# A ninth 2 MB buffer for expert weights in a two-layer hybrid decoder step

## What is computed

```python
def moe(h, router_w, router_bias, w_gate, w_up, w_down):
    score = jax.nn.sigmoid((h @ router_w).astype(jnp.float32))
    ...
    gate = (jax.nn.one_hot(idx, N_EXPERTS, dtype=jnp.float32) * w[..., None]).sum(-2).astype(h.dtype)
    out = jnp.zeros_like(h)
    for e in range(N_EXPERTS):
        hid = jax.nn.silu(h @ w_gate[e]) * (h @ w_up[e])
        out = out + gate[..., e:e + 1] * (hid @ w_down[e])
    return out

def layer_tail(x, mix, p_i, ln1_g, ln1_b, ln2_g, ln2_b, router_w, router_bias, w_gate, w_up, w_down, ple_proj, ple_gate):
    h = layer_norm(DEEPNORM_ALPHA * x + mix, ln1_g, ln1_b)
    h = layer_norm(DEEPNORM_ALPHA * h + moe(h, router_w, router_bias, w_gate, w_up, w_down), ln2_g, ln2_b)
    return h + jax.nn.sigmoid(h @ ple_gate) * (p_i @ ple_proj)
```

## Time and profile before

| | us |
|---|---|
| median of three runs | 1065.74 |
| lowest and highest run | 1064.29, 1072.47 |
| span of the profiled execution | 1061.0 |
| PE busy | 1002.3 (94%) |
| PEld busy | 626.2 (59%) |
| DVE busy | 489.0 (46%) |
| ACT busy | 334.2 (32%) |
| POOL busy | 186.5 (18%) |
| moved by DMA | 343.32 MB, mean 324 GB/s |

### The profile page before, as it was taken

How to read it: one execution, slowest core, us unless ns; L and a number is a source line. 1 busy time by engine, 2 the same in 40 slices (tenths; PEclk the granted TensorE clock), 3 DMA queues, 4 the chain that set the end, 5 groups by cost and what they waited for, 6 DMA issues and landing times. The chain is left out here.

```text
span 1061.0 us, 15018 instructions
## 1 busy us (share of the span) xinstructions
PE 1002.3 (94%) x5207; PEld 626.2 (59%) x5207; DVE 489.0 (46%) x1423; ACT 334.2 (32%) x874; POOL 186.5 (18%) x201
## 2 busy tenths in 40 slices
PE   8999999899999999989999987979999999998997
PEld 6888776688744444433678865445874444443366
DVE  1869898782531111101479896671152111110146
ACT  3211688920351111101241013662045111110134
POOL 0000005330130000000245542441112000000033
PEclk9999999999999999999999996999989999999999
DMA  9844688769669999999837995949966999999975
GB/s 328 289 148 167 175 270 276 244 228 401 255 266 428 425 429 425 427 426 426 342 134 261 385 342 178 333 143 361 424 257 248 424 427 426 427 425 426 429 305 212
DMA packets 89985, 343.32 MB, mean 324 GB/s; under 512 B 15826, under 2 KB 53714, under 8 KB 72978
## 3 DMA queue, kind: packets, MB, share of 16 engines
q1 hardware_dynamic: 79914, 319.58, 77.5%
q10 hardware_dynamic: 7688, 18.39, 4.7%
q0 software_dynamic: 2304, 4.33, 1.2%
HBM read 331.66 MB, written 23.04 MB: 334 GB/s over the span
## 5 line engine op out<-in xcount | busy, mean ns | idle before, releaser
L1517 DVE TENSOR_TENSOR gates_and_hidden<-bank,silu_gate 128x512 f32<-128x512 f32 x16 | 11.1, 691 | 318.0 <-PE bank L1166 318.0
L547 PE MATMUL ss<-xT,expert_ring 128*128 128x264 f32 x384 | 92.4, 402 | 4.3 <-DMA expert_ring<-in_ssd_w_in 4.2
L1166 PE MATMUL bank<-expert_ring,x_packed 128*64 128x512 f32 x384 | 86.8, 596 | 7.4 <-DMA expert_ring<-in_moe_w_up 7.4
L1188 PE MATMUL bank<-expert_ring,gates_and_hidden 128*64 128x512 f32 x384 | 85.0, 595 | 1.4 <-ACT gates_and_hidden L1337 1.4
L547 PEld LDWEIGHTS ss<-xT,expert_ring 128*128 128x128 f32 x384 | 75.0, 198 | 18.7 <-DMA xT<-in_xT 4.2
L1147 PE MATMUL bank<-expert_ring,x_packed 128*64 128x512 f32 x384 | 84.5, 593 | 0.0
L1376 POOL DMA_INDIRECT x_rows_packed<-x_rows,slot_token_int x16 | 16.4, 1023 | 338.3 <-DVE gates_and_hidden L1480 294.7
L1510 DVE TENSOR_TENSOR acc<-acc,bank 128x264 f32<-128x264 f32 x128 | 55.0, 429 | 38.9 <-PE bank L1203 37.3
L1759 PE MATMUL bank<-xT,expert_ring 128*128 128x264 f32 (+1 forms) x324 | 72.5, 386 | 0.3 <-PEq L1000 0.3
L1759 PEld LDWEIGHTS bank<-xT,expert_ring 128*128 128x128 f32 (+1 forms) x324 | 60.3, 187 | 12.4 <-issue 1.0
L1203 PE MATMUL bank<-gates_and_hidden,y_slots 128*128 128x264 f32 x256 | 60.6, 388 | 3.8 <-issue 2.4
(11 more groups left out here) (417 smaller groups left out, 1760.4 us busy)
## 6 DMA issues: line engine op xcount, KB each, us to landing
expert_ring<-in_moe_w_down SPq DMA_DIRECT2D x24, 2048.0 KB, 21.9
expert_ring<-in_moe_w_gate SPq DMA_DIRECT2D x24, 2048.0 KB, 18.2
expert_ring<-in_moe_w_up SPq DMA_DIRECT2D x20, 2048.0 KB, 22.6
expert_ring<-in_ssd_w_in SPq DMA_DIRECT2D x9, 2048.0 KB, 8.0
expert_ring<-in_cmp_pages SPq DMA_DIRECT2D x40, 256.0 KB, 4.5
expert_ring_b<-in_moe_w_gate SPq DMA_DIRECT2D x4, 2048.0 KB, 20.2
expert_ring_c<-in_moe_w_gate SPq DMA_DIRECT2D x4, 2048.0 KB, 24.7
expert_ring<-in_moe_w_up SPq DMA_DIRECT2D x8, 1024.0 KB, 6.7
```

The lines of the kernel that those rows point to most:

```text
L547: last = mm(pt[m % 4][:, 0:T], wc[:, k, ((m - 1) % 4) * P:((m - 1) % 4 + 1) * P], xT[:, k, :], start=k == 0, stop=k == KD - 1)
L1166: last = mm(hb[1][s * CAP:(s + 1) * CAP, :], xg[:, k, s * CAP:(s + 1) * CAP], unit(6 * i + 2 + s)[:, k * FF:(k + 1) * FF], start=k == 0, s ...
L1188: last = mm(ob[2 + a][s * CAP:(s + 1) * CAP, :], ht[:, k, s * CAP:(s + 1) * CAP], unit(6 * i + 4 + s)[:, o:o + 512], start=k == 0, stop=k ...
```

## The change

There are nine buffers: the old eight and a new one, `expert_ring_d`, 16 KB on each partition. It lives only inside a tail, so nothing can be loaded into it before the tail starts. Unit n goes to buffer `n % 9`, by a table `unit_at` that keeps the thirds of the ring apart in another order, and each unit from 9 on waits for the use of unit n - 9. The room comes from three places: the scratch for the dynamic DMA's descriptors is set to 4096 bytes a partition, `silu_gate` goes (silu is written to `hid`, and the product made in place), and `cmp_dec` is allocated for the attention block alone, where the tail's tensors are gone. `log_ev` moves to the start of `x_packed`. The mixer blocks load the same seven buffers at the same waits, filled with other units: 0, 1, 2, 5, 6, 4, 7 ahead of tail 0, and 0, 4, 7, 6, 1, 2, 3 ahead of tail 1.

```diff
+NUNIT = 9
...
-        kcd = keep("cmp_dec", [P, 4, DB, NBP])
...
-            sp.dma_start(dst[:, part], src[:, part]).then_inc(ld_u[n % 8], 16)
+            sp.dma_start(dst[:, part], src[:, part]).then_inc(ld_u[n % NUNIT], 16)
...
         def unit_value(L, n):
-            return 16 * (L * 8 + n // 8 + 1 + (n >= 8)) if n % 8 < 2 else 16 * (L * 6 + n // 8 + 1)
+            pieces = lambda last: sum(2 if m in (NUNIT, NUNIT + 1) else 1 for m in range(n % NUNIT, last + 1, NUNIT))
+            return 16 * (L * pieces(6 * (NE // 2) + 1) + pieces(n))
...
-                sg = sb("silu_gate", [P, FF])
+                ring_d = sb("expert_ring_d", [P, CH])
...
-                log_ev = sg[:, 0:T]
+                log_ev = xg[:].rearrange("p k c -> p (k c)")[:, 0:T]
...
-                unit = lambda n: ring[:, (n % 8) // 3, ((n % 8) % 3) * CH:((n % 8) % 3 + 1) * CH] if n % 8 < 6 else (ring_b[:, 0:CH], ring_c[:])[n % 8 - 6]
+                third = lambda h, c: ring[:, h, c * CH:(c + 1) * CH]
+                unit_at = (third(1, 1), ring_b[:, 0:CH], ring_c[:], third(0, 0), third(0, 1), third(1, 0), third(1, 2), third(0, 2), ring_d[:])
+                unit = lambda n: unit_at[n % NUNIT]
...
-                        load_unit(sp, L, 3 * L, unit(3 * L))
+                        load_unit(sp, L, 3 + 2 * L, unit(3 + 2 * L))
+                        load_unit(sp, L, 8, unit(8))
                         sp.wait_ge(gu_half, L + 1)
-                        for n in (8, 9):
+                        for n in (9, 10):
                             load_unit(sp, L, n, unit(n), slice(0, CH // 2))
                         sp.wait_ge(gu_done, n2 + 1)
-                        for n in (8, 9):
+                        for n in (9, 10):
                             load_unit(sp, L, n, unit(n), slice(CH // 2, CH))
-                        for n in range(10, 6 * NP2 + 2):
-                            i, r = (n - 8) // 6, (n - 8) % 6
+                        for n in range(11, 6 * NP2 + 2):
+                            i, r = (n - NUNIT) // 6, (n - NUNIT) % 6
...
                             if i >= 1:
-                                act.wait_ge(hid_ok, n1 + i)
-                            A_(sg[:], hb[0][:], ACT.Silu).then_inc(silu_ok, 1)
+                                act.wait_ge(turned, n1 + i)
+                            A_(hid, hb[0][:], ACT.Silu).then_inc(silu_ok, 1)
...
-                        A_(sg[0:1, FF - 1:FF], epst[0:1, 0:1], ACT.Sigmoid)
+                        A_(gto[0:1, 0:1], epst[0:1, 0:1], ACT.Sigmoid)
...
-                            if i >= 1:
-                                dve.wait_ge(turned, n1 + i)
-                            V.tensor_tensor(hid[:], hb[1][:], sg[:], ALU.mult).then_inc(hid_ok, 1)
+                            V.tensor_tensor(hid, hb[1][:], hid, ALU.mult).then_inc(hid_ok, 1)
...
+            kcd = sb("cmp_dec", [P, 4, DB, NBP])
...
-    nc = bacc.Bacc("TRN2", target_bir_lowering=False, num_devices=1)
+    nc = bacc.Bacc("TRN2", target_bir_lowering=False, num_devices=1, dynamic_dma_scratch_size=4096)
```

More of the change, by code:

```diff
@@ L87, in trunk @@
         dve_step, act_step, pool_step = (Chain(sem(n)) for n in ("dve_step", "act_step", "pool_step"))
-        ld_const, ld_u = sem("ld_const"), [sem(f"ld_unit{n}") for n in range(8)]
+        ld_const, ld_u = sem("ld_const"), [sem(f"ld_unit{n}") for n in range(NUNIT)]
         ld_chunk = [sem("ld_chunk0"), sem("ld_chunk1")]
@@ L343, in _ @@
                     sp.wait_ge(st_done, NG)
-                    load_unit(sp, 0, 4, ring[:, 1, CH:2 * CH])
+                    load_unit(sp, 0, 0, ring[:, 1, CH:2 * CH])
                     sp.wait_ge(st_taken, NG)
@@ L349, in _ @@
                     sp.wait_ge(ms_done, NG)
-                    load_unit(sp, 0, 6, ring_b[:, 0:CH])
+                    load_unit(sp, 0, 1, ring_b[:, 0:CH])
                     store_state(6)
@@ L353, in _ @@
                         sp.wait_ge(st_out[n], 16 * (DB // 4))
[L354 removed]
+                    load_unit(sp, 0, 2, ring_c[:])
                     store_state(7)
@@ L359, in _ @@
                     sp.wait_ge(st_out[2], 16 * (DB // 4))
-                    load_unit(sp, 0, 3, ring[:, 1, 0:CH])
+                    load_unit(sp, 0, 5, ring[:, 1, 0:CH])
                     sp.wait_ge(st_out[3], 16 * (DB // 4))
                     sp.wait_ge(stored, n_stored[0])
-                    load_unit(sp, 0, 5, ring[:, 1, 2 * CH:3 * CH])
+                    load_unit(sp, 0, 6, ring[:, 1, 2 * CH:3 * CH])
                     for n in (1, 2):
                         sp.wait_ge(w_read, n + 1)
-                        load_unit(sp, 0, n, ring[:, 0, n * CH:(n + 1) * CH])
+                        load_unit(sp, 0, 3 * n + 1, ring[:, 0, n * CH:(n + 1) * CH])
                     sp.wait_ge(conv_out, 32)
@@ L1717, in _ @@
                     sp.wait_ge(kv_used, 10)
-                    load_unit(sp, 1, 4, kv_buf[4])
+                    load_unit(sp, 1, 0, kv_buf[4])
                     for n in (1, 2):
                         sp.wait_ge(kv_used, 10 + n)
-                        load_unit(sp, 1, n, kv_buf[n])
+                        load_unit(sp, 1, 3 * n + 1, kv_buf[n])
                     sp.wait_ge(stored, n_stored[0])
@@ L1724, in _ @@
                     load_ple(sp, 1)
-                    load_unit(sp, 1, 5, chunk[2])
-                    load_unit(sp, 1, 6, ring_b[:, 0:CH])
-                    load_unit(sp, 1, 7, ring_c[:])
+                    load_unit(sp, 1, 6, chunk[2])
+                    load_unit(sp, 1, 1, ring_b[:, 0:CH])
+                    load_unit(sp, 1, 2, ring_c[:])
                     sp.wait_ge(o_done, od0 + 4)
-                    load_unit(sp, 1, 0, kv_buf[0])
+                    load_unit(sp, 1, 3, kv_buf[0])
                 @block.gpsimd
@@ L2071, in compress @@
                         dve_step(dve, cmp_multiply(V, b, 1))
-                        cmp_sum(V, b, 0)
-                        cmp_sum(V, b, 1)
+                        cmp_sum(V, kcd, b, 0)
+                        cmp_sum(V, kcd, b, 1)
                         dve.wait_ge(c_mult, 2 * b)
-                        cmp_sum(V, b, 2)
-                        cmp_sum(V, b, 3).then_inc(c_used, 1)
+                        cmp_sum(V, kcd, b, 2)
+                        cmp_sum(V, kcd, b, 3).then_inc(c_used, 1)
                     dve.wait_ge(ld_cmp[cmp_slot(0)], 16 * NPG)
@@ L2082, in _ @@
                     for a in range(4):
-                        i1 = cmp_sum(V, 0, a)
+                        i1 = cmp_sum(V, kcd, 0, a)
                     i1.then_inc(c_used, 1)
```

4 lines of the change are left out of this document (2 added, 2 removed).

## The result

The changed kernel takes 1057.34 us in the median of 20 runs (1048.43 to 1065.74), the kernel before 1064.29 us in the median of 20 runs taken beside them. The ratio is 0.9933, with a 95% interval from 0.9914 to 0.9953: about 7 us less, within 1%. Forecast were 1055.9 us and a gain of 9.8 us, from a median before of 1065.74 us.

What follows compares the result with a forecast made beforehand. The prediction took the transfer queue for expert weights to bound the expert stages. One 4.91 us unit less in each of two layers gave 9.8 us, other terms 0: 1065.74 - 9.8 = 1055.9 us, range 1050.5 to 1061.

Steps and rivals of the forecast that it cites:

- The bound and the count: Expert stages: their end is set by units still to load after gu_half, times 4.91 us; one fewer per layer.
- What PE makes of it: PE's waits on expert weights fall from 13.25 to about 3.4 us, none at pair 5; time falls 9.8 us.
- rival (a): PE's clock falls may vanish (1051.4 us, chance 0.16) or appear in layer 0 (1060.4, 0.16 shared with rival (b)).
- Silu in place, the moves, the scratch: In-place silu, moved router logits and cmp_dec, and 4096-byte dynamic-DMA scratch: each taken as 0 us.
- Rival (d): Row gathers go in rounds because of the short descriptor ring: about 1175 us; chance 0.05 with anything like it.
- rival (c): Queue starved later in the expert stages by SP held on a wait, giving the lead back: 1065.7 us; chance 0.09.
- Where unit 8 lies: Tail starts: free in layer 0; in layer 1 over the x_rows writes, taken as 0, at most 1.0 us.
- rival (b): Layer 1: writes or gather late beyond the slack, 1057 to 1060.8 us; chance 0.16 shared with rival (a) slower.

Runs made afterwards that it cites:

- first execution: First profiled execution of the changed kernel, nothing else altered: span 1059.4 us, against 1061.0 us for the kernel before.
- room only: Kernel before with the shorter scratch, silu in place, the moves of log_ev and cmp_dec, and the new buffer allocated but never used: 0.9999.
- one dummy load: room only plus a 2 MB load into the unused buffer at each tail's start, its data read by nobody: 1.0027 against the kernel before.
- change, second: Profile from a repeat group of runs of the changed kernel, nothing altered; that group measured 0.9940 against the kernel before.
- change, third: Profile from another repeat group of the unaltered changed kernel, on a third chip; that group measured 0.9930 against the kernel before.
- behind_rows: Changed kernel with unit 8 issued only when the three x_rows writes have landed: 0.9945 against the kernel before.
- late_in_layer_1: Changed kernel with unit 8 issued at once in layer 0, but behind the first two gathers in layer 1: 0.9895 against the kernel before, 1054.96 us.

## Why the prediction was right, point by point

**The bound and the count: right.** "Units still to load after `gu_half`, times 4.91 us" gave 4.91 us a layer. The first execution has 5.45 and 5.49, the mean of three 5.1, and the removal of one unit from the old kernel 3.9 and 5.2. From `gate(1)` to `up(7)` of layer 1 it is 170.3 us for 175.6. No wait grew behind `up(7)`: rest of the span 60.66 against 60.07.

**What PE makes of it: right in place, too small in size.** No wait at pair 5 and, in the first execution, none at pair 6; one at pair 7. The forecast left 1.4 us in layer 1 and 0.2 + 1.8 in layer 0, measured are 2.60 and 0.42 + 2.77, the 0.42 before `gate(7)`. In the two other executions 0.67 and 0.33 us are left at `up(6)` of layer 1. From `gate(0)` on, PE was ready for `up(7)` of layer 1 after 192.3 us, where the sum had 194.0 (994.60 - 800.57): the clock's fall at 972 to 976, priced at 1.7 us, had gone with the wait ahead of it, as rival (a) thought it might. The weights came after 194.9 us, where the sum had 195.4. So the wait is longer and the stage isn't: the end is the transfer's, and the 1.7 us were worth nothing, as forecast. In the changed kernel's chain of waits (start us, us, what) the last stage of layer 1 still leaves PE for a weight:

```profile
963.08 6.89 PE bank L1151 x32
969.99 28.61 DMA expert_ring<-in_moe_w_up
998.74 7.09 PE bank L1170 x32
```

One such piece instead of two.

**Silu in place, the moves, the scratch: right.** 0 forecast, 0.9999 measured for all of them together. Rival (d) falls with it, and rival (c) by the stages, which are 5.1 us shorter. DVE's waits before its product are 310.1 us over both layers and all put down to PE, as the earlier trace rows led to expect:

```profile
L1519 DVE TENSOR_TENSOR gates_and_hidden<-bank,gates_and_hidden 128x512 f32<-128x512 f32 x16 | 11.1, 692 | 310.1 <-PE bank L1170 310.1
```

**Where unit 8 lies: the step that failed.** For layer 0 "free" was right: in all three executions of the change DVE releases the gather there, 18.3 us after the start. For layer 1 the cost was taken as 0, with 1.0 us as the bound above, on this: the gather is "released by DVE and not by the writes" and has 3.9 us of slack (4.1 without the rounding). True of the trace before, but a release says only which of two waits ended last there. The write was the other one, and the forecast had no term for it: the bound shifted only the gather's own landing by a unit. It also took from one execution that the queue is idle when the writes go out. The traces show that this differs. The table has, for layer 1, what SP's queue moved in the 12 us from the first write's issue, and when the slots from DVE were ready and the gather went out (us after the tail's start):

| execution | SP's queue, MB | DVE ready | gather issued |
|---|---|---|---|
| before | 0.02 | 17.45 | 18.25 |
| change, first | 1.26 | 18.44 | 19.48 |
| room only, no added load | 1.34 | 17.55 | 19.61 |
| one dummy load | 2.36 | 17.59 | 22.52 |
| change, second | 2.47 | 19.14 | 25.24 |
| change, third | 3.38 | 17.45 | 24.15 |

In all but the first the write is named as the release. The more SP's queue still has to move, the longer the gather waits behind DVE: 0.8, 1.0, 2.1, 4.9, 6.1 and 6.7 us. The unit adds up to 2.1 MB, and what the attention block has left over adds from 0 to 1.3 MB, so a delay can be longer than the unit's own 4.91 us; the first execution, with a short remainder, stands no worse than room only, which has no unit 8 there. PE idles 0, 5.83 and 3.32 us before the transposes in the three executions of the change. So rival (b) happened, beside the forecast's own gain, and took about 3 us, the 10.2 of the stages against 7.0 in the medians; this size has an error of some 2 us.

In the first execution layer 1's chain of waits changed too. Before, it came to PE's L1053 over DVE's ranking of the experts:

```profile
785.12 0.22 DVE insel L1450
...
786.57 1.16 PE bank L1053 x4
```

Now it comes to the same matmuls (L1057) over ACT and its writes:

```profile
785.40 1.25 ACT y_slots L1298 x2
...
786.68 1.27 ACTq L1301
...
787.99 0.40 ACT ple_projected L1285
...
788.43 1.16 PE bank L1057 x4
```

From the tail's start that is 16.00 us instead of 15.27. Issuing the third write holds ACT for 1.27 us, and `ple_projected` and PE are late by it. In ACT's timeline of the kernel before the same issue takes 0.52:

```profile
785.55 0.52 ACTq L1297 DMA_DIRECT2D x_rows<-y_slots  x1
```

Unit 8 isn't shown to be the cause of that: the same issue took 0.52 us in the change's two other executions, 0.78 in room only and 1.00 in one with the unit held behind the gathers.

The Trainium skill (DMA: Bandwidth & Descriptors, "Issuing engines are not separate DMA queues") says that transfers interleave on the same 16 engines, whoever issues them. The traces agree: the writes are ACT's and the loads SP's, and with the dummy load the gather went out at 22.5 us instead of 19.6 in room only.

**The clock, rival (a): it happens, and the runs don't show it as the change's doing.** The slower form of rival (a), a fall in layer 0, came in the first execution. Router phase 0 fell to 0.82 and took 29.3 us in two of three executions of the change, and in `behind_rows`; it took 24.7 in the third, and in `late_in_layer_1`, which has the same loads there. None of the six profiles of kernels that work with eight buffers has a fall there, but six are too few to rule out that the change makes it more frequent. Router phase 1 took 24.5 to 29.6 us in kernels with no added load ahead of the first gather's landing. The part between `up(7)` and tail 1, which the change hardly touches, took 271.7, 272.1 and 277.2 us in three executions of the changed kernel. Such steps of 4 to 5 us are why one profiled execution (1059.4 against 1061.0) tells so little here. They come and go in both kernels: over 88 runs of the kernel before the mean granted clock and the time go together with a correlation of -0.87, and the mean granted clock is 0.974 for both kernels.

**The sum.** 10.2 us in the expert stages, 0 for the room, some 3 back in router phase 1: 7 us. The forecast of 9.8 was near because the larger term was right; its error is the collision. That 1055.9 us lies only 1.4 us from the measured 1057.34 is in part luck: the median of three runs that it started from was 1.4 us above the median of twenty, and that hid half of the 2.8 us by which the gain was too large.

What stays open: why the attention block leaves more in SP's queue in one execution than in another, and why `behind_rows` doesn't gain.

## What to carry to other kernels

Where a saturated queue sets the end of a stage, a prefetch is worth the bytes that it moves out of the saturated stretch into an idle one; count units and not waits, and expect little from a buffer alone (1.7 us a layer here) and more from the moment at which its load starts (3.4 us more). Before putting such a load into a stretch that looks idle, list every small transfer there and all that its readers wait for, also the waits that end first today: the trace shows only the last. If there is one, try the large load behind the last of them, as long as its own due time allows: behind the writes alone it gained nothing over the immediate load (0.9945), behind the gathers too it probably did. And look at more than one execution before calling a stretch idle: the same stretch held 0.02 MB of SP's loads in one and 1.34 in another.

## What the runs showed of the hardware

Three small writes (264 rows of 4 KB together) land the later the more SP's queue of large loads still has to move: with 0.02 MB in the 12 us from the first write's issue they are done before DVE's value is, and with 1.26, 1.34, 2.36, 2.47 and 3.38 MB the gather behind them goes out 1.0, 2.1, 4.9, 6.1 and 6.7 us after that value. A load of 2.097 MB (4.91 us at 427 GB/s) in their way can so cost a transfer behind them more than its own time.

With one more unit in SP's queue at `gu_half` the stretch behind `up(0)` went from 409 and 406 GB/s to 429.

The same instructions in router phase 0 took 24.7 or 29.3 us, at a granted clock of 1.00 or 0.82, in executions of one kernel.

A dynamic-DMA scratch of 4096 bytes a partition was enough for gathers of 144 packets, at most two of them under way: 0.9999 (0.9972 to 1.0025).
